# Value products of a retrieval layer on 32-column quarters of TensorE, gathers of four slots by 32 tokens

## The reference

```python
h2 = rms_norm(x1) * gain
q = (h2 @ wq).reshape(tokens, 8, 128)
v1, i1 = top_k(q[..., :64] @ k1.T, 16)
v2, i2 = top_k(q[..., 64:] @ k2.T, 16)
sc, pos = top_k(all sums of v1 and v2, 16)
idx = 128 * i1 + i2, at pos
g = softmax(sc)
pre = einsum('td,thkd->thk', h2, u[idx])
act = gelu(pre) * g
out = einsum('thk,thkd->td', act, v[idx])
x2 = x1 + out
y = final_norm(x2 + sigmoid(norm(x2) @ w_gate) * (p @ w_proj))
```

## Time and profile before

| | |
|---|---|
| three runs, median | 4762.41 us |
| lowest, highest | 4756.2, 4764.85 us |
| span of the profiled execution | 4754.3 us |
| the profiled execution's own time beside its span | not given |
| instructions | 50461 |
| PE busy (matmuls) | 4255.9 us, 90% |
| DVE busy | 3116.5 us, 66% |
| ACT busy | 996.5 us, 21% |
| POOL busy | 1481.0 us, 31% |
| moved by DMA | 1379.14 MB, 1166.48 MB of it by the queue of the gathers |
| mean granted TensorE clock | 0.958 |

### The profile page before, as it was taken

One profiled execution on the slowest core, in us unless ns is written; L12 is line 12 of the kernel. 1 busy time (PEld: TensorE's weight loads), 2 busy tenths in 40 slices (PEclk: granted clock), 3 DMA queues, 4 the chain that ended last, 5 costly groups with the idle time before them and its releaser, 6 DMA issues.

```text
span 4754.3 us, 50461 instructions
## 1 busy us (share of the span) xinstructions
PE 4255.9 (90%) x16837; PEld 2643.1 (56%) x16837; DVE 3116.5 (66%) x7138; ACT 996.5 (21%) x2580; POOL 1481.0 (31%) x1391
## 2 busy tenths in 40 slices
PE   8999999999898889888888999778988888888878
PEld 8999777888765675445443555323433433434332
DVE  3444113666377538887789777677777777777784
ACT  2222111234266301110111111111212111212212
POOL 1100002222111003444444444444444444444442
PEclk8999999999899999999999999999999999999999
DMA  2223222344323359999999999999999999999996
GB/s 93 69 89 124 88 91 75 123 129 129 110 77 109 113 180 369 396 413 410 417 405 409 403 416 405 420 420 403 409 409 419 385 402 416 397 416 408 383 413 259
DMA packets 310425, 1379.14 MB, mean 290 GB/s; under 512 B 37856, under 2 KB 112336, under 8 KB 175024
## 3 DMA queue, kind: packets, MB, share of 16 engines
q0 software_dynamic: 167728, 1166.48, 60.6%
q1 hardware_dynamic: 142464, 209.70, 12.8%
HBM read 1295.58 MB, written 80.49 MB: 289 GB/s over the span
## 4 chain that ended last, share of the span: by engine, by line
PE 31%; DMA 19%; DVE 10%; issue 4%; POOL 1%; ACT 0%; DVEq 0%; ACTq 0%; POOLq 0%
DMA peer_uv<-in_peer_uv_dram,peer_idx 19%; PE peer_acc L2740 19%; PE peer_fo L2675 4%; PE peer_fo L2688 2%; PE peer_fo L2576 2%; DVE peer_uv L2000 2%; PE peer_tb L2520 2%; DVE peer_diag L2030 1%; DVE peer_hot L1958 1%; DVE peer_hot L1961 1%; POOL peer_uv L1864 1%; DVE peer_sel L1964 1%; PE peer_fo L2594 0%; PE peer_acc L2624 0%; DVE peer_pos L1948 0%
## 5 line engine op out<-in xcount | busy, mean ns | idle before, releaser
L2740 PE MATMUL peer_acc<-peer_uv,peer_diag 128*128 128x512 f32 (+1 forms) x4000 | 1932.3, 622 | 303.5 <-DVE peer_diag L2030 296.3
L1864 POOL DMA_INDIRECT peer_uv<-in_peer_uv_dram,peer_idx x1056 | 1232.5, 1167 | 1704.5 <-PE peer_acc L2740 1577.2
L2000 DVE CUSTOM_DVE_ANT_0 peer_uv<-peer_uv,peer_h 128x1024 f32<-128x1024 f32 x1056 | 1290.7, 1222 | 639.9 <-DMA peer_uv<-in_peer_uv_dram,peer_idx 637.7
L2740 PEld LDWEIGHTS peer_acc<-peer_uv,peer_diag 128*128 128x128 f32 (+1 forms) x4000 | 742.3, 195 | 1285.5 <-issue 727.3
L2479 ACT ACTIVATE peer_ge<-peer_pre 128x1 f32<-128x1 f32 x1056 | 212.8, 203 | 2425.7 <-DVE peer_pre L2000 2425.1
L2675 PE MATMUL peer_fo<-peer_space 128*128 128x256 f32 (+2 forms) x1152 | 395.6, 475 | 42.0 <-DVE peer_space L2094 16.9
L99 PE MATMUL proj_bank<-proj_hTh,proj_wplead 128*128 128x352 f32 x1008 | 357.7, 355 | 1.8 <-DVE proj_wprest L91 1.8
L2030 DVE TENSOR_SCALAR peer_diag<-ident,peer_ge,peer_gw 128x128 f32<-128x128 f32 x968 | 332.2, 343 | 9.7 <-ACT peer_ge L2479 7.4
L2675 PEld LDWEIGHTS peer_fo<-peer_space 128*128 128x128 f32 x1152 | 221.7, 197 | 204.9 <-issue 157.8
L100 PE MATMUL proj_bank<-proj_hTr,proj_wplead 128*128 128x352 f32 x1008 | 328.8, 326 | 0.0
L101 PE MATMUL proj_bank<-proj_hTh,proj_wprest 128*128 128x352 f32 x1008 | 328.6, 326 | 0.0
(11 more groups left out here) (370 smaller groups left out, 5418.0 us busy)
## 6 DMA issues: line engine op xcount, KB each, us to landing
proj_wp<-in_w_in_dram POOLq DMA_DIRECT2D x13, 2048.0 KB, 9.8
peer_space<-in_w_ssm_o_dram SPq DMA_DIRECT2D x48, 512.0 KB, 7.6
peer_uv<-in_peer_uv_dram,peer_idx POOLq DMA_INDIRECT x1056, 12.1
proj_wp<-in_w_in_dram POOLq DMA_DIRECT2D x14, 1024.0 KB, 8.3
peer_space<-in_w_attn_o_dram SPq DMA_DIRECT2D x24, 512.0 KB, 7.9
peer_space<-in_w_out_dram SPq DMA_DIRECT2D x24, 512.0 KB, 7.8
scratch_xtok<-proj_shared SPq DMA_DIRECT2D x20, 512.0 KB, 3.2
scratch_chan<-proj_stg SPq DMA_DIRECT2D x48, 176.0 KB, 1.8
```

The lines of the kernel that those rows point to most:

```text
L1864: pool.indirect_dma_start(uv[k][:], None, io["peer_uv"], bass.IndirectOffsetOnAxis(ap=idx[t % 2][:, col:col + 1], axis=0)).then_inc(uv_in[ ...
L2000: dve.tensor_tensor_reduce(uv[k][:, 0:D], uv[k][:, 0:D], h2[t % 2][:], 1.0, 0.0, ALU.mult, ALU.add, pre[g % 2][:, k:k + 1]).then_inc(u_don ...
L2740: x = pe.matmul(acc[0:r, h:h + HALF], diag[k][:, 0:r], uv[k][:, D + h:D + h + HALF], start=(it == 0 and k == 0), stop=False)
```

## The change

- A gather holds four slots of 32 tokens: partition quarter `copy` holds slot 4a + copy, all for token group j (tokens 32j to 32j + 31 of the tile), and the groups take turns, j = n % 4. `idx` and `gw` are written in that order by 16 instructions each in place of one.
- The rows of h2 stand in four tiles `rep[j]`: in each, token group j four times. TensorE makes them by 32 matmuls of 512 columns for a tile (`replicate`), ScalarE copies them out of PSUM (`rep_copy`), in the last step of the tile before.
- The stationary matrix is `fold` scaled to 128x32 (`scaled`) in every tile, and the product goes to the rows 32j to 32j + 31 of `acc` (`value`).
- No product is done aside any more.
- `h2` has one buffer (`KEPT` = 1), `x1` lies in `hT` and loads at slot 80, `s12` holds 4 heads, so the second scores come at step 12 (9 for the last tile, 14 for tile 2).
- The last tile's `place_copies` and its four loads of h2 go.

```diff
-    PE_AHEAD, POOL_BEHIND = 3, 7
+    PE_AHEAD, POOL_BEHIND = 3, 5
...
-    KEPT = 2
+    KEPT = 1
...
-    ASIDE_TILES, ASIDE_FROM, ASIDE_EVERY = 2, 2, 4
...
+    def handled(n):
+
+        return n + 1
+
+    def second_scores(t):
+
+        return 14 if LATE[t] else 9 if t == LAST else 12
+
+    def rep_place(t, j):
+
+        return ((acc[:, 0:HALF], acc[:, HALF:D]) if t == 0 and j % 2 == 0 else
+                [x[:].rearrange("p k n -> p (k n)") for x in (sb_ if t and j % 2 else tb)])
+
+    def copies_of(t):
+
+        return QUAD if t < LAST else 1
...
                     sp.wait_ge(h2_stored, h2_stores(group_of(t)))
-                    for copy in range(0, P, r):
-                        sp.dma_start(h2[t % 2][copy:copy + r, :], dr["h2"][tokens(t, r), :]).then_inc(h2_in[t % 2], 16)
+                    sp.wait_ge(rep_made, QUAD * t)
+                    sp.dma_start(h2[0:r, :], dr["h2"][tokens(t, r), :]).then_inc(h2_in, 16)
...
                     sp.wait_ge(x1_stored, 16 * OFF[group_of(t) + 1])
+                    if t < LAST:
+                        sp.wait_ge(prep_pe, (t + 1) * PREP_PE + 5)
+                    else:
+                        sp.wait_ge(closed, t)
...
-                    if at == 2 and t:
-                        sp.wait_ge(closed, t)
+                    if at == (SLOTS * 10 if t < LAST else 2):
                         load_x1(t)
...
-                        if aside(n - SLOTS):
-                            pool.wait_ge(aside_done, asides[n - SLOTS])
-                        else:
-                            pool.wait_ge(v_done, products(n - SLOTS))
+                        pool.wait_ge(v_done, handled(n - SLOTS))
...
+                def placed(x, t, p, j, copy):
+
+                    n = PTOP // QUAD * 2 * copies_of(t)
+                    return x[t % 2][quarter(copy), p * n:(p + 1) * n].rearrange("r (e a j) -> r e a j", e=2, j=copies_of(t))[:, :, :, j]
...
-                        dve.scalar_tensor_tensor(out=idx[t % 2][:, 2 * p * PTOP:(2 * p + 2) * PTOP].rearrange("p (e a) -> p e a", e=2),
-                                                 in0=sel[:, :, 0, :], scalar=float(PNK), in1=sel[:, :, 1, :],
-                                                 op0=ALU.mult, op1=ALU.add).then_inc(tk, 1)
+                        for j, copy in quarters(t):
+                            x = dve.scalar_tensor_tensor(out=placed(idx, t, p, j, copy), in0=taken_from(sel[:, :, 0, :], j, copy), scalar=float(PNK),
+                                                         in1=taken_from(sel[:, :, 1, :], j, copy), op0=ALU.mult, op1=ALU.add)
+                        x.then_inc(tk, 1)
...
+                    n = g * SLOTS + k
+                    q, j = n // QUAD, n % QUAD
+                    if n % PSLOT < copies_of(t):
+                        dve.wait_ge(rep_out, QUAD * t + j + 1)
                     dve.wait_ge(uv_in[k], g * 16 + 16)
-                    dve.tensor_tensor_reduce(uv[k][:, 0:D], uv[k][:, 0:D], h2[t % 2][:], 1.0, 0.0, ALU.mult, ALU.add,
-                                             pre[g % 2][:, k:k + 1]).then_inc(u_done, 1)
+                    dve.tensor_tensor_reduce(uv[k][:, 0:D], uv[k][:, 0:D], rep[j % copies_of(t)][:], 1.0, 0.0, ALU.mult, ALU.add,
+                                             pre[q % 2][:, j:j + 1]).then_inc(u_done, 1)
...
+                    if n >= 2 * QUAD:
+                        dve.wait_ge(v_done, handled(n - 2 * QUAD))
...
+                    dve.wait_ge(gelu_done, handled(n))
+                    j = n % QUAD
+                    dve.tensor_scalar(scaled[q % 2][:, j, :], fold[:], ge[q % 2][:, j:j + 1], gw[t % 2][:, col:col + 1],
+                                      ALU.mult, ALU.mult).then_inc(scaled_done, 1)
...
+                def rep_copy(t, j):
+                    n = QUAD * t + j
+                    act.wait_ge(rep_made, n + 1)
                     if t:
+                        act.wait_ge(u_done, t * PSLOT - QUAD + j + 1)
+                    for h, place in enumerate(rep_place(t, j)):
+                        x = act.activation(rep[j][:, h * HALF:(h + 1) * HALF], place, ACT.Copy)
+                    x.then_inc(rep_out, 1)
...
+                            if t < LAST and it == ITS - 1 and k == SLOTS - 1:
+                                for copy in range(copies_of(t + 1)):
+                                    if copy < 2:
+                                        rep_copy(t + 1, copy)
...
+                        if it == ITS - 1 and t < LAST - 1:
+                            for copy in range(2, QUAD):
+                                rep_copy(t + 1, copy)
...
+                def replicate(t, j):
+
+                    n = QUAD * t + j
+                    if j == 0:
+                        pe.wait_ge(prep_act, (t + 1) * PREP_ACT if t else 6)
+                    elif j >= 2:
+                        pe.wait_ge(rep_out, n - 1)
+                    for h, place in enumerate(rep_place(t, j)):
+                        for copy in range(QUAD):
+                            x = pe.matmul(place[copy * DEC:(copy + 1) * DEC, :], c.ident[:, j * DEC:(j + 1) * DEC],
+                                          h2[:, h * HALF:(h + 1) * HALF], start=True, stop=True)
+                    x.then_inc(rep_made, 1)
...
+                for j in range(QUAD):
+                    replicate(0, j)
                 for time in range(T0, PE_AHEAD):
                     mixing(time)
+
+                def value(n, t, g, it, k):
+
+                    at = n % copies_of(t) * DEC
+                    if n < QUAD:
+                        pe.wait_ge(rep_out, QUAD)
+                    pe.wait_ge(scaled_done, handled(n))
+                    pe.wait_ge(uv_in[k], g * 16 + 16)
+                    for h in range(0, D, HALF):
+                        x = pe.matmul(acc[at:at + DEC, h:h + HALF], scaled[n // QUAD % 2][:, n % QUAD, :],
+                                      uv[k][:, D + h:D + h + HALF], start=(it == 0 and k < copies_of(t)), stop=False)
+                    x.then_inc(v_done, 1)
...
-                            if not aside(n):
-                                pe.wait_ge(diag_done, products(n))
-                                pe.wait_ge(uv_in[k], g * 16 + 16)
-                                for h in range(0, D, HALF):
-                                    x = pe.matmul(acc[0:r, h:h + HALF], diag[k][:, 0:r], uv[k][:, D + h:D + h + HALF],
-                                                  start=(it == 0 and k == 0), stop=False)
-                                x.then_inc(v_done, 1)
+                            if t < LAST and it == ITS - 1 and k in (1, 6):
+                                for j in range(copies_of(t + 1)):
+                                    if j // 2 == (k == 6):
+                                        replicate(t + 1, j)
+                            value(n, t, g, it, k)
```

152 lines of the change are left out of this document (65 added, 87 removed).

## The result

The changed kernel takes **4859.53 us** (median of four runs, 4857.18 to 4860.96), the kernel before on the same chip 4762.4: 1.0208 times as long, 95% interval 1.0194 to 1.0222 (ratios here are estimated over all runs; the two medians alone give 1.0204). Forecast was 4862. The profiled execution has a span of 4859.4 us, 105.1 more than before's. The sum came out nearly right; its parts did not, and the rest of this document is about them.

What follows compares the result with a forecast made beforehand. The gather queue was taken as the bound, with TensorE close behind in tiles 0 to 2. Tiles 0 to 2 +50, +30, +25, start +8, tiles 3 to 7 -10: +103, given as 4862 us; range 4800 to 4940, wider 4770 to 5000.

Steps and rivals of the forecast that it cites:

- asides to TensorE: Tiles 0 and 1: the 56 products VectorE added aside go to TensorE at 1.72 us, +48 us of work each.
- switch, without overlap: TensorE going to full-width work and back costs 0.31 us each time: 36, 38 and 33 us in tiles 0 to 2.
- overlap: Neighbouring products in different column quarters save 0.43 us a pair: 5, 3 and 9 us in tiles 0 to 2.
- placing in 16 pieces: VectorE index and weight placing: 3 us a pair, 12 us a tile, covered by its idle time.
- replicas of tiles 1 to 7: Repeated rows made on TensorE in the last eight slots of the tile before: 7 us a tile.
- replicas ahead of slot 0: Tile 0's repeated rows, made on TensorE right before its first product: +8 us straight.
- Tiles 3 to 7: Of 55 us lost to a dry queue, overlap returns 20 and boundaries take 10: -10 us.
- tiles 4 to 7 differ by more than 10 us each: Sign for wrong: it would put the cause at the tile boundary and not in the switch.
- Signs: Right: tile 0 at least 420 us, period 3.3 us, replicas in fours; wrong: neighbouring products together, TensorE busy time falls.
- The first (quarters never overlap): Rival: products and replicas in different column quarters run one after the other; about 5025 us, chance 0.20.
- the second: Rival: faster, the switch isn't paid and waiting products run side by side; about 4705 us, chance 0.11.
- The third (it evens out): Rival: switches fall in TensorE's idle time, dense stretches give the rest back; within 0.2% (10 us), chance 0.05.

Runs made afterwards that it cites:

- experiment 1: Kernel before with all products on TensorE, none done aside on VectorE: 4765.23 us against 4760.87, ratio 1.0011.
- experiment 2: Kernel before without asides, each product cut to 32 columns, quarters by turns, three quarters of the sum left out: 4787.35 us, ratio 1.0059.
- experiments 2 and 3: Kernel before without asides, 32-column products, three quarters of the sum left out: quarters by turns 4787.35 us; always the first quarter 4835.62 us.
- experiment 5: Changed kernel with one VectorE instruction for a pair's indices and one for its weights, in tiles 0 to 7: 4802.71 us, ratio 1.0092 to before.

## Why the prediction was right in its sum and wrong in its parts

The loss of 97 us by the runs, each part against the kernel that lacks it:

| part | predicted | measured |
|---|---|---|
| asides to TensorE | +48 us of work in tiles 0 and 1 each | +4 us in time |
| switch, without overlap | 36, 38, 33 us of TensorE | +70 us |
| overlap | -17 (tiles 0 to 2), -20 later | -48 us |
| placing in 16 pieces | 0 (3 us a pair, covered) | +57 us |
| replicas of tiles 1 to 7 | +7 a tile within tiles 0 to 2, 10 in all later | +19 us |

They add up to 102 us. The first three are taken on the kernel before, the last two on the changed one, so they needn't add exactly to 97. The order counts too: the asides were returned first, to a TensorE with idle time, and used it up before the switch was added. In another order asides would likely cost more and the switch less; no run has it. The replicas ahead of slot 0 were forecast at +8; the first gather starts 4.8 us later, and no run tests them alone.

- **The failed step** is "3 us a pair, 12 us a tile", costed at nothing because VectorE is idle 67 us and more in each of tiles 2 to 7 and relieved of 40 in tiles 0 and 1. Its size was wrong: the earlier trace rows shows two small instructions 0.09 us apart and also 0.17 us long, and I took only the first as price, which pieces that keep their quarter also show; these change quarters each time and took 0.178 each. Its cover was wrong as well, and weighed more: VectorE's idle time is waiting for landings, spread at some 1 us a slot, and sixteen pieces in a row at the end of the longest segment meet none of it: 57 us in the runs where the sum had 0. By the bound I named (12 us a tile where nothing covers it) the term could have been 96 us; I had put it in the range, not in the sum.
- **Asides.** The +48 us was rightly counted as work, and the division by 0.96 held: TensorE was 96% busy in tile 0 both in experiment 1 (390.08 of 405.40) and in the changed kernel (399.40 of 414). Tile 0 was forecast +50 and came +30 because the work came out 12 us under even the low end of its sum, 411, by the two terms below (in tile 0 experiment 2 has 408.09 us of work against 390.08 in experiment 1: 18 us, where 36 - 5 = 31 were forecast). In experiment 1 it came +10, since TensorE had 40 us idle there and the clock rose.
- **Overlap** was mis-sized at 0.43 us a pair; it is 1.72, the upper bound that I had kept. Products side by side also arise after VectorE's bursts, which my count of neighbouring slots left out. In tiles 0 to 2 I had 17 us of work saved; experiments 2 and 3 differ by 36.
- **Switch.** 0.31 us there and back was exact. But 107 us was counted for tiles 0 to 2, and TensorE's busy time rose there by 79; the time of the whole kernel rose by 70. My estimate is that the other switches fall where TensorE stands idle before the product.
- **Tiles 3 to 7** were forecast -10 and came +22, +16 of it in tile 3. My own sign "tiles 4 to 7 differ by more than 10 us each would put the cause at the boundary" was blind to this: they differ by under 5 us each, and pieces (by experiment 5: 9.5, 11, 3, 4) and overlap nearly cancel there.
- **Signs.** Of those for right, the period of 3.32 us and the replicas in fours came; tile 0 is 96% busy but 414 us long in its window, 425 from gather to gather, with the queue at 369 GB/s. One sign for wrong came too: over the whole run TensorE's busy time fell, from 4255.9 to 4219.0 us, since products run beside each other in tiles 3 to 7; in tile 0 it rose.
- **Rivals.** The first (quarters never overlap) is refuted by the 1.92 us row. Of the second the overlap half came true and the unpaid switch did not. The third (it evens out) is refuted by the 97 us. Range and direction held. That the sum met the result within 3 us is luck: tiles 0 to 2 were forecast +105 and came +78, tiles 3 to 7 were forecast -10 and came +22, the start +8 and came +5. Switch and overlap together were put too high, the pieces left out, and the errors cancelled.

## What to carry to other kernels

Small instructions in a row on an engine that feeds a ring can cost by the length of the burst, though the engine is idle a fifth of the time: compare the burst with the slack of one slot, and spread it or shrink it. Price a small instruction by a row that shares its partition pattern; one that changed quarter cost twice one that stayed. And freeing the busiest engine by reordering gave nothing here, where what it held back was the ring's buffer: check first whether its new idle time would be a wait for the engine behind it in the loop, and what clock it then runs at.

## What the runs showed of the hardware

- Two fp32 products in different column quarters, issued whole one after the other, ran in 1.92 us together against 1.90 us alone. Between a 128-column and a 32-column product, there and back cost 0.31 us (3.32 against 3.01 us a period). The Trainium skill, TensorEngine Tiling, Key Properties, says that a change of mode drains TensorE. The 0.31 us agrees with such a drain, though no row shows the drain itself.
- VectorE: 16 pieces of 32x8 took 1.70 us within their quarter and 2.85 us when moved from quarter to quarter: 0.08 to 0.09 us from start to start where the quarter stays, 0.17 to 0.18 where it changes.
- In tiles 3 to 5 of the changed kernel the granted clock was 0.90 to 0.91, against 0.96 before: a mean of the two levels (0.91 is some 18% of the time at 1.2 GHz and the rest at 2.4). TensorE was idler there: 258.06 us busy of 342 in tile 4, against 294.52 of 336. In tile 3 the clock fell from 1.00 to 0.53 behind a wait of 6.64 us. No run here tells what the lower clock cost in all.
